# Twelve-stage transformer block: each joint of stages passed one 128-row tile at a time, with GpSimd making two low weight halves

## What is computed

```python
def rms_norm(x, g):
    xf = x.astype(jnp.float32)
    y = xf * lax.rsqrt(jnp.mean(xf * xf, axis=-1, keepdims=True) + EPS)
    return (y * g.astype(jnp.float32)).astype(x.dtype)
...
    for i in range(DEPTH):
        g = norm_g[i]
        f = swiglu(rms_norm(x, g[0]), ffn_w_in[i, 0], ffn_w_out[i, 0])
        x = x + FFN_RESIDUAL_WEIGHT * rms_norm(f, g[1])
        h = rms_norm(x, g[2])
...
        x = x + rms_norm(m, g[3])
        f = swiglu(rms_norm(x, g[4]), ffn_w_in[i, 1], ffn_w_out[i, 1])
        x = x + FFN_RESIDUAL_WEIGHT * rms_norm(f, g[5])
```

## Time and profile before

| | |
|---|---|
| median of 3 runs | 1805.64 us |
| span of the profiled execution | 1799.2 us |
| PE (TensorE matmul) busy | 1686.5 us, 94% |
| PEld (weight load, beside PE) busy | 1526.8 us |
| DVE (VectorE) busy | 954.5 us, 53% |
| ACT (ScalarE) busy | 765.1 us, 43% |
| POOL (GpSimd) busy | 51.2 us, 3% |
| chain that ended last | PE 89%, DVE 7%, ACT 2% |
| mean granted TensorE clock | 0.951 |

### The profile page before, as it was taken

The page is one execution under the profiler, slowest core; times in us unless marked ns, Lnnn a source line. Parts: engine busy times, 40 slices in busy tenths (PEclk is TensorE's granted clock), DMA queues, the critical chain, the costliest instruction groups (busy, mean ns, idle before and its releaser), DMA issues.

```text
span 1799.2 us, 24875 instructions
## 1 busy us (share of the span) xinstructions
PE 1686.5 (94%) x10554; PEld 1526.8 (85%) x10554; DVE 954.5 (53%) x950; ACT 765.1 (43%) x866; POOL 51.2 (3%) x120
## 2 busy tenths in 40 slices
PE   8999899889998999879899999979998889899997
PEld 7999797689998999868899988869997767799985
DVE  5444554454445445456544454575556644655565
ACT  5334534544335433436543344234444324434442
POOL 1000000000000000020000001000000010000000
PEclk9999999989999999989999999989999895899998
DMA  8555451255554555430555545346555440365551
GB/s 277 183 188 185 157 183 45 78 169 187 187 187 152 185 189 185 134 109 9 176 187 187 187 152 165 117 134 205 187 187 170 151 159 1 115 204 187 189 188 47
DMA packets 187694, 282.68 MB, mean 157 GB/s; under 512 B 5671, under 2 KB 142494, under 8 KB 187486
## 3 DMA queue, kind: packets, MB, share of 16 engines
q1 hardware_dynamic: 184702, 271.29, 45.5%
q0 software_dynamic: 2912, 10.24, 1.8%
HBM read 280.46 MB, written 1.05 MB: 156 GB/s over the span
## 4 chain that ended last, share of the span: by engine, by line
PE 89%; DVE 7%; ACT 2%; issue 1%; POOL 1%; DMA 0%; SPq 0%; DVEq 0%; POOLq 0%; ACTq 0%
PE wk L547 15%; PE wk L549 15%; PE wk L548 15%; PE acc L547 12%; PE acc L548 11%; PE acc L549 11%; PE wk L562 1%; PE wk L766 1%; PE wk L759 1%; PE wk L564 1%; PE wk L758 1%; PE wk L855 1%; ACT weights_high L1011 1%; DVE weights_low L1298 1%; DVE x_rows L1666 1%
## 5 line engine op out<-in xcount | busy, mean ns | idle before, releaser
L1298 DVE TENSOR_TENSOR weights_low<-weights_raw,weights_high 128x2048 fp32r<-128x2048 f32 x258 | 590.6, 2294 | 504.3 <-ACT weights_high L1011 504.3
L1011 ACT ACTIVATE weights_high<-weights_raw 128x2048 fp32r<-128x2048 f32 x258 | 492.1, 1911 | 442.5 <-PE acc L549 274.1
L547 PE MATMUL wk<-turned_high,weights_high 128*128 128x256 f32 x2128 | 605.4, 285 | 6.6 <-DVE weights_low L1298 4.7
L548 PE MATMUL wk<-turned_low,weights_high 128*128 128x256 f32 x2128 | 604.2, 284 | 0.0
L549 PE MATMUL wk<-turned_high,weights_low 128*128 128x256 f32 x2128 | 604.1, 284 | 0.0
L547 PEld LDWEIGHTS wk<-turned_high,weights_high 128*128 128x128 f32 x2128 | 410.3, 193 | 11.1 <-DVE weights_low L1298 6.2
L548 PEld LDWEIGHTS wk<-turned_low,weights_high 128*128 128x128 f32 x2128 | 410.3, 193 | 2.5
L549 PEld LDWEIGHTS wk<-turned_high,weights_low 128*128 128x128 f32 x2128 | 410.2, 193 | 0.0
L547 PE MATMUL acc<-weights_high,hidden_high 128*128 128x512 f32 x608 | 237.8, 391 | 0.1
L548 PE MATMUL acc<-weights_low,hidden_high 128*128 128x512 f32 x608 | 237.5, 391 | 0.0
L549 PE MATMUL acc<-weights_high,hidden_low 128*128 128x512 f32 x608 | 236.6, 389 | 0.0
(11 more groups left out here) (259 smaller groups left out, 1204.0 us busy)
## 6 DMA issues: line engine op xcount, KB each, us to landing
weights_raw<-ffn_w_in_dram SPq DMA_DIRECT2D x88, 1024.0 KB, 5.1
weights_raw<-ffn_w_out_dram SPq DMA_DIRECT2D x44, 1024.0 KB, 5.0
weights_raw<-mlp_w_up_dram SPq DMA_DIRECT2D x32, 1024.0 KB, 5.4
weights_raw<-mlp_w_down_dram SPq DMA_DIRECT2D x32, 1024.0 KB, 4.9
weights_raw<-sb_w_in_dram SPq DMA_DIRECT2D x12, 1024.0 KB, 5.2
weights_raw<-a_w_in_dram SPq DMA_DIRECT2D x12, 1024.0 KB, 5.2
weights_raw<-ple_w_gate_dram SPq DMA_DIRECT2D x8, 1024.0 KB, 5.0
weights_raw<-sb_w_out_dram SPq DMA_DIRECT2D x4, 1024.0 KB, 5.0
```

The lines of the kernel that those rows point to most:

```text
L547: nc.tensor.matmul(dst, lh, rh, start=first, stop=False)
L548: nc.tensor.matmul(dst, lh, rl, start=False, stop=False)
L1011: A(whi[:, u % RING, :], raw[:, u % RING, :], ACT.Copy).then_inc(high_ready, 1)
L1298: V.tensor_tensor(wlo[:, u % RING, :], raw[:, u % RING, :], whi[:, u % RING, :].bitcast(F32), ALU.subtract).then_inc(unit_ready, 1)
```

## The change

At each of the eleven joints, tile 0 goes alone. The new stage's units U+1 and U+2 (the "edge" units) get their own semaphores: their high halves are made by ScalarE or VectorE inside the joint (`edge`, and a copy in `leave_rms`), and their low halves by GpSimd (`edge_low`). TensorE turns tile 0, multiplies it with the first unit, turns tile 1, multiplies tile 0 with the second unit, then tile 1 with both (`open_rows`). To let a single tile pass, the opening of FFN and MLP is computed with the rows stationary (`group_rows`, 256 weight columns a matmul, result in `acc`), and the hidden values are then turned (`turn_hidden`, four transposes a hidden group). The MLP's order of units changes: both first up-units come first and each down-unit follows two steps behind. The sb stage now splits the next stage's first unit itself (`split_to(U + 17)` for `U + 16`). The last RMS joint, before mLSTM, turns tile 0 in the middle of the previous stage's last products (`between`). The PLE rows are turned at the end of the MLP.

```diff
+            def edge_low(s, U):
+
+                for e in (1, 2):
+                    u = U + e
+                    pool.wait_ge(edge_high[e - 1], s)
+                    nc.gpsimd.tensor_tensor(wlo[:, u % RING, :], raw[:, u % RING, :], whi[:, u % RING, :].bitcast(F32),
+                                            ALU.subtract).then_inc(edge_ready, 1)
...
+            def open_rows(u, part, turn_second):
+
+
+                for t in range(T):
+                    for j in range(2):
+                        if t == 0 and j:
+                            turn_second()
+                        if t == 0:
+                            wait_unit(u + j)
+                        mm = part(j, t)
+                        if t:
+                            mm.then_inc(unit_done, 1)
...
+            def leave_rms(s, half, U, m, gain, scaled):
+
+                act.preload_act_table_set("sqrt_and_others")
+                act.wait_ge(result, s)
+                root_mean_square(acc[:, 0, :], 0, 0, half)
+                if scaled:
+                    act.wait_ge(x_ready, T * s - 1)
+                    root_mean_square(x[:, 0, :], 0, 4)
+                else:
+                    keep_turned(m, gain, 0)
+                act.wait_ge(unit_done, U)
+                root_mean_square(acc[:, 1, :], 1, 1, half)
+                if scaled:
+                    keep_turned(m, gain, 0)
+                edge(U, 2)
+                if scaled:
+                    act.wait_ge(x_ready, T * s)
+                    root_mean_square(x[:, 1, :], 1, 5)
+                keep_turned(m, gain, 1)
...
+                weighted(0)
+                inverse(0)
+                add(0)
+                u = U + 1
+                dve.wait_ge(landed[u % RING], 16 * (u // RING + 1))
+                dve.wait_ge(unit_done, u - RING + 1)
+                V.tensor_copy(whi[:, u % RING, :], raw[:, u % RING, :]).then_inc(edge_high[0], 1)
+                if scaled:
+                    scale_rows(0)
+                else:
+                    keep_turned(m, gain, 0)
+                weighted(1)
+                inverse(1)
+                if scaled:
+                    keep_turned(m, gain, 0)
+                add(1)
+                if scaled:
+                    scale_rows(1)
+                keep_turned(m, gain, 1)
...
-                for t in range(T):
-                    row = x[:, t, :]
-                    wait_result(s, end, t)
-                    chain.link(V.scalar_tensor_tensor(row, row, ALPHA if bias is None else 1.0, acc[:, t, :], ALU.mult, ALU.add))
...
+                chain.link(add(0))
+                normalize(0)
+                chain.count(add(1))
+                keep_turned(m, None, 0)
+                dve.wait_ge(dve_chain, chain.n)
+                normalize(1)
+                keep_turned(m, None, 1)
```

More of the change, by code:

```diff
@@ L286, in build @@
         p_loaded = sem("ple_rows_loaded")
-        ple_s = {n: sem("ple_" + n) for n in ("turned", "high", "kept", "biased", "gate", "projected")}
+        ple_s = {n: sem("ple_" + n) for n in ("turned", "high", "kept", "biased", "gate", "projected", "times")}
         ple_rows = work[:, 12800:13312].rearrange("p (t n) -> p t n", t=T)
@@ new lines, in turn_mixed, with turn @@
+                mix_fresh[0] = o
+            def turn(m, src, ready, t, scaled=False):
+                pe.wait_ge(*ready(t))
+                for k in range(KD):
+                    dst = wk[:, k // 2, t * S + (k % 2) * P:t * S + (k % 2 + 1) * P]
+                    rows = src[:, t, k * P:(k + 1) * P]
+                    if scaled:
+                        mm = nc.tensor.matmul(dst, rows, scales[:, t, :], start=True, stop=True)
+                    else:
+                        mm = nc.tensor.transpose(dst, rows, ident[:, :])
+                    if k % 2:
+                        mm.then_inc(turned, 1)
+                fresh[t] = m
@@ L588, in down_tile, with turn_hidden @@
+            def turn_hidden(bank, rows):
+                for k in range(2):
+                    for t in range(T):
+                        mm = nc.tensor.transpose(wk[:, bank, k * S + t * P:k * S + (t + 1) * P], rows(k, t), ident[:, :])
+                mm.then_inc(hidden_turned, 1)
             def down_tile(u, b, t, first, last):
@@ L672, in ffn @@
                         down(r - 1, 0)
[L673 to L686, removed]
+                last_down(U + 3 * FG - 2, H + FG - 1, 2, FG - 2, between)
@@ L1003, in _ @@
             A = nc.scalar.activation
-            next_unit = [0]
+            next_unit, sums = [0], [0]
             def split(u, i=0):
@@ new lines, in leave_ple @@
+            def leave_ple(n, U, m):
+                act.preload_act_table_set("sigmoid_and_others")
+                for t in range(T):
+                    act.wait_ge(ple_s["biased"], T * n + t + 1)
+                    A(xn[:, t, :], xn[:, t, :], ACT.Sigmoid).then_inc(ple_s["gate"], 1)
+                if U < TOTAL:
+                    edge(U, 1)
+                    keep_turned(m, None, 0)
+                    edge(U, 2)
+                    keep_turned(m, None, 1)
+                    next_unit[0] = U + RING
@@ new lines, in _, with wait_std, scale_rows, wait_result @@
+            stds = [0]
+            def wait_std():
+                stds[0] += 1
+                dve.wait_ge(std_ready, stds[0])
+            def scale_rows(t):
+                wait_std()
+                y = stat[:, 32 + t:33 + t]
+                chain.link(V.reciprocal(y, stat[:, 6 + t:7 + t]))
+                V.tensor_scalar(scales[:, t, :], ident[:, :], y, None, ALU.mult).then_inc(scales_ready, 1)
+            def wait_result(s, U, t):
+                if t == 0:
+                    dve.wait_ge(result, s)
+                else:
+                    dve.wait_ge(unit_done, U)
```

576 lines of the change are left out of this document (346 added, 230 removed).

## The result

The changed kernel takes 1828.35 us (median of 4 runs, 1825.74 to 1831.05) against 1805.04 us (4 runs) of the kernel before: ratio 1.0129, 95% interval 1.0114 to 1.0143. It is slower by 23 us, and the forecast was 1828.0. The profiled span grew from 1799.2 to 1826.3 us.

A forecast was written before the change was run, and what follows sets the result against it. TensorE, busy 94% of the span, bounds the kernel. Terms 13.2 - 4.1 + 5 + 12.8 - 3.4 - 2.5 + 2.1 = +23.1 take the span from 1799.2 to 1822, median 1828 us (+1.3%); range 1790 to 1842.

The forecast's parts named there:

- GpSimd's 4.55 us: Each joint's two GpSimd subtractions over 128 x 2048: 4.55 us each, shutting out certain VectorE operations that long.
- RMS joints: Joints 1, 3, 4 and 5: equivalent start 19.6 against 16.3, +3.3 us each, plus 1 each for the clock.
- The blocked diagonal: In RMS joints VectorE's diagonal waits for GpSimd's subtraction: tile 0's mean near 4 us in place of 0.29.
- Second joint: Sb stage now makes the first unit's low half: 19.6 against 23.7, -4.1 us, plus 1 for the clock.
- Layer-norm joints: Joints 7, 8, 10, 11: VectorE's norm of tile 1 waits for GpSimd; +4.5, +1.9, 3.2 and 3.2, together +12.8 us.
- The rest: Turning hidden values +3.6, start +0.7, end -1.2, MLP down-units two steps behind -1.0: together +2.1 us.
- Sixth: Sixth joint: no VectorE operation on two SBUF tensors falls into GpSimd's time; 10.0 against 13.4, -3.4 us.
- ninth: Ninth joint: loses part of its gain to one wait of 2 us; -2.5 us, bounds -4.6 and 0.
- The start: Kernel's start: unit 1's low half comes behind the keeping of tile 0, +0.7 us.
- the hidden turns: Turning hidden values in 4 FFNs and 2 MLPs: 32 transposes at 0.08 to 0.16 us each, +3.6 us.
- Rival (a): Diagonals pass; only operations with two tensors from SBUF wait: -13 us in total, 1793 us; chance 22%.
- Rival (b): GpSimd costs VectorE nothing: total about -43 us, 1762 us; chance 8%.

The follow-up runs named there:

- the summing form: Changed kernel with VectorE's diagonal tensor_scalar also writing out each row's sum to an unread accumulator: 1782.36 us, ratio 0.9879 to the kernel before.
- norms behind: Changed kernel with each GpSimd subtraction waiting for its tile's x, only outside the RMS joints: 1807.86 us, ratio 1.0017 to the kernel before.
- before, unit 17: Kernel before, with only the sb stage also making the first unit of the FFN behind it: 1798.02 us, ratio 0.9966.
- vector lows: Changed kernel with the 22 low halves of the edge units moved from GpSimd to VectorE: 1773.17 us, ratio 0.9818 to the kernel before.
- GpSimd behind: Changed kernel with each GpSimd subtraction waiting until its tile's own operation on VectorE has run: 1768.41 us, ratio 0.9797 to the kernel before.

## Why the prediction was right

The mechanism and the total came as forecast; the terms less exactly.

- *GpSimd's 4.55 us.* 22 rows, 4.49 us at the least, mean 4.87 since several, those outside the RMS joints above all, waited for VectorE themselves. The copy took 1.22 (1.25 expected).
- *The blocked diagonal* was the one cost that no row of before showed. It read 4.06, and tile 1's ended 20.4 us after tile 0's result (20.5 expected). The choice was right, and the summing form shows that it is the plain form of the instruction that waits. The argument for it was thin: that a cast of 96 columns in SBUF takes 49 ns less than a copy of 99 from PSUM can have other causes, and no run tested it.
- *RMS joints.* Expected with their clock 4.3 each for 1, 3, 4 and 5; measured +8.0, +4.5, +7.2, +5.6. The third and fifth are right. Of the first's, several us lie in the sb attention's clock: with the same joints, "norms behind" has 154.6 there against 159.0, and with the code of before, "before, unit 17" has 155.4 against 151.0. The fourth's +7.2 repeats (122.1 in three profiles) and was mis-sized: TensorE has the clock 0.50 over 774 to 778 and again over 786 to 790, 0.76 and 0.67 between; 1 us for the clock was too little there.
- *Second joint*: -3.1 expected, -1.7 measured. Unit 17 alone gives -6.5, the order and the gates take 4.8 back, as in the third.
- *Layer-norm joints.* Seventh +3.9 (4.5 expected), tenth +3.6 (3.2). Eighth -0.2 and eleventh -0.1, where 1.9 and 3.2 stood: the step that failed. I had tile 1's first fused operation come due at 4.6 after the end of tile 0's norm, just behind the start of GpSimd's second subtraction, wait for it to 9.1, and the norm end at 11.9. It came due at 3.9, before the first subtraction was over at 4.5, so it went next; the second subtraction waited for it, and only the last fused operation stood behind that, with 5.20 where the forecast had one operation near 5.8. The norm ended at 11.0 in all four. The other part is the clock: of the 1.6 of slowed products behind the turn only some 0.7 came in the eighth, where the first five take from 1430.08 to 1431.91 and those after them 0.23 each. In the eleventh the kernel before had itself the clock 0.50 over 1759 to 1763 and 0.65 over 1763 to 1767, the changed one 0.50 over 1793 to 1797 and then 0.99; the mean of the seventh and eighth left that out.
- *The rest.* Sixth -2.2 (-3.4), ninth -3.1 (-2.5), end -1.4 (-1.2). The start cost 3.1 and not 0.7: behind TensorE's idle after the turn of tile 0 the clock is 0.67 over 14 to 18, where the profile of before has 1.00; in "vector lows", with the same code there, it stays at 1.00 and the start costs 1.6. The turns of hidden values were not run by themselves; the FFN stretch of "vector lows" is 3.7 under that of before with them in it.

Added up: the four RMS terms were 8.1 too small, the second joint's 1.4, the start's 2.4, the sixth's 1.2; the layer-norm terms were 5.6 too large and the ninth's 0.6. The 2.6 for the hidden turns and the MLP's order lie inside these stretches. That is how +23.1 became +27.1 between the two profiled spans. About 4 us of it may not be the change at all. Every timed run on record is 1.7 to 2.1 us above its own span, so the 1799.2 of before stands for a time near 1801, under the four timed ones (1804.28 to 1806.57), and its sb attention is the one with 151.0 where the same code took 155.4. So of the 6.4 between median and span only 2 lie before the first and after the last instruction; the changed kernel's median is 2.0 above its span. Timed against timed the change costs 23.3, and that this meets the forecast so closely is luck: single joints were off by up to 3.7 us, and their signs cancelled in part.

Rival (a) is what the summing form makes real: the diagonals pass, and the kernel takes 1782 (1793 was worked out). Rival (b), GpSimd at no cost, is nearly "GpSimd behind" with 1768 (1762). What the extra turns of hidden values cost, and why the fourth joint's clock falls lower than the third's, stays open.

## What to carry to other kernels

Before giving GpSimd a long elementwise operation, look at what VectorE does in that time: operations with two tensors from SBUF and a plain one-tensor `tensor_scalar` stood still here until it ended; those with PSUM on one side, the statistics and small reciprocals passed. What decides is the place on the path to TensorE's next product and the length of one instruction, not the sum of the work: start the long operation behind the critical one, cut it into pieces, or give the critical one a form that passes. And when a wait is priced, price the slower products behind it too.

## What the runs showed of the hardware beyond that

- The hand-over comes at the end of each instruction of GpSimd, also within a run of them: 0.83 us for a diagonal issued 0.5 us after the first of four pieces of 1.25 began. GpSimd waits too: 4.92 for its 4.5 where VectorE's add was running.
- In the sliding-window attention TensorE is busy all the time and has the lower clock for over 40 us, before the change as after. A window of the kernel before:

```profile
1490.00:1530.00 40.00, 40.00 (x149) 31.55 (x147) 17.75 (x52) 16.83 (x57) 0.00 (x0) 0.50 0.00 1
```

No run here touched it, and why the clock stays low there is open. An estimate: 40 us at 0.50 hold the work of 20 us at 1.00, so up to 20 us lie in these 40 alone, about as much as the whole change cost.
